# Eighteen input tiles of the even layer as split products, their low weights and the convolutions redistributed over four engines

## The chip, the cores and the metric

The kernel runs on one core of one Trainium2 chip. It is written for the engines directly: five instruction queues (TensorE, VectorE, ScalarE, GpSimd and SyncE) run in their own order and meet only at semaphores. The metric is the device time of one execution in microseconds. The kernel before takes 1738.14 us, the median of 3 runs (1737.71 to 1739.41).

## What is computed

The reference is one step of a two-layer encoder on 640 frames (a prompt of 512 frames, and 8 requests of 16 frames). The change lies in the front of the first (even) layer:

```python
proj = h @ w_in                      # h = rmsnorm(x), [640, 1024]
a_val, a_gate, z, xbc, dt_raw = split(proj)   # 512, 512, 512, 1024, 8 columns
a_glu = a_val * sigmoid(a_gate)
a_conv, new_conf_state = causal_dwconv(a_glu, conf_state, conf_w, conf_b)    # 31 taps, 512 channels
a_out = silu(layernorm(a_conv, ln_g, ln_b))
xbc_c = silu(causal_dwconv(xbc, ssd_conv_state, xbc_w, xbc_b))               # 4 taps, 1024 channels
...
y = ssd_scan(xs, dt, a, b_in, c_out, h0);  yg = y * silu(z);  b_out = rmsnorm(yg)
out = concat([a_out, b_out]) @ w_out
```

A convolution sees each request with its own carried-in frames, so the 512 prompt columns and the 8 x 16 request columns of a channel are separate pieces. The two runs over the memory tokens (keys `mk`, values `mv` of both layers) are computed between these projections.

## The kernel before

Everything lies channel-major: 128 channels on the partitions, 640 frames along them. A projection tile is 128 output channels by 640 frames, summed over 8 blocks of 128 input channels. Tiles alternate between two PSUM buffers `G[0]` and `G[1]`; `TILE` numbers them in the order of TensorE, and `begin(n)` waits until tile n-2 has been read. Weights arrive in chunks of two tiles in a ring of four slots, loaded by the SyncE queue in a fixed order.

Two kinds of product occur. `project` (called by `projections`) multiplies the f32 weights with the f32 rows `h`; each k-block takes a matmul of 512 and one of 128 columns, and the profile shows two records for each, 32 for a tile. The split product, used from `evout` tile 2 on, adds three products of rounded parts (high by high, low by high, high by low) in fp32r, 48 matmuls of 320 columns for a tile. It needs high and low parts of weights and rows: ScalarE copies to fp32r (high), and VectorE or GpSimd subtracts (low).

The order of TensorE in the stage of the change (written out by hand in `block.tensor`): the eight `glu` tiles (gate and value alternately), the narrow tile `dtp`, the four key tiles `mk1` with a statistic after each from the second on, `dt`, the two value tiles `mv1`, the eight `xbc` tiles with `conv_stat(3)` after the sixth, two `z` tiles, `conv_stat(6)`, the tile `tok`, two more `z` tiles, and the scan. All 22 tiles of glu, xbc, z and the narrow ones read `h`.

VectorE (`block.vector`) forms the four gated blocks (L2446, L2447), and in between the taps of the 31-tap convolution in `conv_taps`: for each channel block and tap one `scalar_tensor_tensor` on the 512 prompt columns and one on the 128 request columns, accumulating in `acc` in SBUF (L2434). Two instructions that follow each other never depend on each other; each waits for the one two before it. After that come `conv_sum` (L2463), the four taps of the `xbc` convolution per block (L2515, L2518) in `tmp`, again in both pieces, `subtract_mean`, and `decay_sums` (L2473 to L2496). ScalarE applies the silu of each `xbc` block (`xbc_silu`, which releases `tmp`), reads the `xbc` tiles (`xbc_rows`), the `z` tiles (`z_gate`), and works through the key statistics in `head_norms`. GpSimd scales the keys (`memory_keys`, L779 and L781) and stores the carried-out convolution states (L761).

## Time and profile before

| what | value |
|---|---|
| time, median of 3 runs | 1738.14 us (1737.71 to 1739.41) |
| span of the profiled execution | 1735.7 us |
| TensorE busy | 1702.0 us, 98% |
| VectorE busy | 1058.7 us, 61% |
| ScalarE busy | 683.9 us, 39% |
| GpSimd busy | 370.5 us, 21% |
| granted TensorE clock, mean | 1.000 |

The span runs from the first to the last instruction of one execution; 2.4 us of the median lie outside of it. Busy times are unions over the span. The length of an instruction in a row is from its start to its end, and on ScalarE and VectorE the next may start before that end, so a run of n instructions in one row gives their pitch: the row's length less the last one's, over n-1.

### The profile page before, as it was taken

How to read it: one execution, taken by the hardware profiler on the slowest of the kernel's cores; microseconds unless marked ns; L12 is line 12 of the kernel's file. 1: busy time of each engine (PE TensorE's matmuls, PEld its weight loads, DVE VectorE, ACT ScalarE, POOL GpSimd, SP SyncE). 2: the span in 40 equal slices, each digit the busy share in tenths (PEclk: the TensorE clock that was granted, in tenths of full speed). 3: DMA queues.
4: the chain of work that ended last, by engine and by line, in shares of the span. 5: the costliest groups of instructions: out<-in, count | busy, mean ns of one | idle time of the engine just before them, and what ended most of it. 6: DMA issues, size and time to landing. Idle time of an engine off the chain costs nothing.

```text
span 1735.7 us, 27688 instructions
## 1 busy us (share of the span) xinstructions
PE 1702.0 (98%) x11360; PEld 1543.0 (89%) x11360; DVE 1058.7 (61%) x1717; ACT 683.9 (39%) x1219; POOL 370.5 (21%) x289
## 2 busy tenths in 40 slices
PE   7999998999999999999999999999999999999999
PEld 6566556797999999999989899789899999999999
DVE  3699867637667647465654424744676774655574
ACT  4111243435525525253552124633543453544352
POOL 3012100211104324132213132200110241414240
PEclk9999999999999999999999999999999999999999
DMA  8222330142303131403143221603320313122212
GB/s 263 101 77 103 93 107 28 49 195 98 104 27 138 32 130 46 135 19 128 31 141 74 75 73 64 246 27 114 153 93 25 128 48 115 61 70 86 87 66 91
DMA packets 39674, 162.30 MB, mean 94 GB/s; under 512 B 9384, under 2 KB 10280, under 8 KB 25600
## 3 DMA queue, kind: packets, MB, share of 16 engines
q1 hardware_dynamic: 32240, 124.59, 21.5%
q0 software_dynamic: 7312, 35.98, 5.8%
q8 instruction: 89, 1.46, 0.4%
q14 instruction: 33, 0.27, 0.0%
HBM read 149.87 MB, written 10.42 MB: 92 GB/s over the span
## 4 chain that ended last, share of the span: by engine, by line
PE 92%; DVE 5%; ACT 2%; issue 1%; DMA 0%; POOL 0%; SPq 0%; DVEq 0%; ACTq 0%
PE G L940 68%; PE S L940 11%; PE Q L940 11%; PE Q L1635 1%; ACT work L1731 0%; DVE rstd L2344 0%; DMA ring<-in_w_mk 0%; DVE ev_low L2593 0%; ACT rstd L1731 0%; DVE stats L2623 0%; DVE resid L2875 0%; ACT h_split L1731 0%; PE Q L1347 0%; DVE stats L2992 0%; DVE work L2636 0%
## 5 line engine op out<-in xcount | busy, mean ns | idle before, releaser
L940 PE MATMUL G<-ffn_rows,w_split 128*128 128x320 f32 x2160 | 329.8, 309 | 0.0
L940 PEld LDWEIGHTS G<-ffn_rows,w_split 128*128 128x128 f32 x2160 | 320.1, 188 | 0.0
L1731 ACT ACTIVATE w_split<-ring 128x512 fp32r<-128x512 f32 (+2 forms) x224 | 159.1, 711 | 316.8 <-PE G L940 208.4
L940 PE MATMUL G<-front,ring 128*128 128x128 f32 (+2 forms) x832 | 223.3, 430 | 11.0 <-DMA ring<-in_w_mk 9.3
L940 PEld LDWEIGHTS G<-front,ring 128*128 128x128 f32 x832 | 133.0, 193 | 100.0 <-issue 95.9
L856 POOL TENSOR_TENSOR mkT<-ring 128x512 f32<-128x512 f32 x72 | 98.2, 1369 | 564.6 <-DMA ring<-in_w_up 382.2
L940 PE MATMUL G<-h_split,w_split 128*128 128x320 f32 x1344 | 200.9, 310 | 1.2 <-DVE w_split L2359 0.8
L940 PEld LDWEIGHTS G<-h_split,w_split 128*128 128x128 f32 x1344 | 197.5, 188 | 1.9 <-issue 1.3
L940 PE MATMUL G<-g_split,w_split 128*128 128x320 f32 x1056 | 163.7, 310 | 0.1
L940 PEld LDWEIGHTS G<-g_split,w_split 128*128 128x128 f32 x1056 | 156.7, 188 | 1.7 <-DVE w_split L2848 1.4
L2715 DVE TENSOR_TENSOR w_split<-ring,w_split 128x512 fp32r<-128x512 f32 (+1 forms) x124 | 105.8, 854 | 59.9 <-ACT w_split L1731 58.7
L2848 DVE TENSOR_TENSOR w_split<-ring,w_split 128x512 fp32r<-128x512 f32 (+1 forms) x80 | 66.9, 837 | 115.5 <-ACT w_split L1731 114.7
L2434 DVE SCALAR_TENSOR_TENSOR front<-front,par 128x512 f32<-128x512 f32 x240 | 113.6, 549 | 0.1
L1731 ACT ACTIVATE work<-G 128x320 f32<-128x320 f32 (+1 forms) x116 | 53.0, 457 | 141.2 <-PE G L940 138.5
L2715 DVE TENSOR_TENSOR w_split<-mv,w_split 128x512 fp32r<-128x512 f32 x72 | 50.4, 700 | 54.9 <-ACT w_split L1731 54.9
L940 PE MATMUL S<-g_split,w_split 128*128 128x320 f32 x528 | 82.1, 309 | 0.5 <-DVE w_split L2848 0.5
L940 PE MATMUL Q<-g_split,w_split 128*128 128x320 f32 x528 | 81.1, 309 | 0.1
L1731 ACT ACTIVATE front<-G 128x640 f32<-128x640 f32 (+3 forms) x44 | 24.4, 573 | 142.0 <-PE G L940 142.0
L940 PEld LDWEIGHTS S<-g_split,w_split 128*128 128x128 f32 x528 | 78.5, 188 | 0.8 <-DVE w_split L2848 0.8
L940 PEld LDWEIGHTS Q<-g_split,w_split 128*128 128x128 f32 x528 | 78.3, 188 | 0.3 <-DVE w_split L2848 0.3
L870 POOL TENSOR_TENSOR w_split<-ring,w_split 128x1024 fp32r<-128x1024 f32 x18 | 43.5, 2415 | 121.9 <-ACT w_split L1731 121.9
L940 PE MATMUL S<-ffn_rows,w_split 128*128 128x320 f32 x432 | 69.2, 309 | 0.0
(351 smaller groups left out, 2818.8 us busy)
## 6 DMA issues: line engine op xcount, KB each, us to landing
ring<-in_w_up SPq DMA_DIRECT2D x44, 1024.0 KB, 4.8
ring<-in_w_down SPq DMA_DIRECT2D x48, 256.0 KB, 2.6
ring<-in_w_down SPq DMA_DIRECT2D x32, 320.0 KB, 2.9
front<-in_mem_k POOLq DMA_DIRECT2D x8, 1024.0 KB, 6.1
front<-in_mem_v POOLq DMA_DIRECT2D x8, 1024.0 KB, 10.6
ring<-in_w_mk SPq DMA_DIRECT2D x4, 1024.0 KB, 5.9
ring<-in_w_mv SPq DMA_DIRECT2D x4, 1024.0 KB, 10.9
ring<-in_w_glu SPq DMA_DIRECT2D x4, 1024.0 KB, 8.6
```

Source lines behind the costliest of these rows:

```text
L856: nc.gpsimd.tensor_tensor(wsum[n], a, b, ALU.subtract).then_inc(sum_ready, 1)
L870: nc.gpsimd.tensor_tensor(lo, src, hi.bitcast(F32), ALU.subtract).then_inc(split, 1)
L940: return nc.tensor.matmul(out, lhsT, rhs, start=start, stop=stop, **kw)
L1635: m = nc.tensor.transpose(Q[0:z - a, e, a:a + P], fP[it % 2][:, e, a:z], ident)
L1731: return nc.scalar.activation(*a, **k)
L2434: ins = v.scalar_tensor_tensor(out=out, in0=src, scalar=tap, in1=out, op0=ALU.mult, op1=ALU.add)
L2715: v.tensor_tensor(lo, src, hi.bitcast(F32), ALU.subtract).then_inc(op_low, 1)
L2848: v.tensor_tensor(lo, src, hi.bitcast(F32), ALU.subtract).then_inc(split, 1)
```

## The change

- **Split tiles.** `FRONT` lists 18 tiles: the last six `glu` tiles, all `xbc`, all `z`, numbered q = 0 to 17. `front_product(q)` computes them as split products. The first two `glu` tiles and `dtp` stay as they were, and `dtp` moves ahead of the six. The high rows `in_hi` are a ScalarE copy of `h` into the room of the residual `x`; the low rows are `h - in_hi`, on VectorE, in place of `h`, after `dtp` has read it. `x` is fetched again from HBM by the SyncE queue after the last `z` tile (four transfers), and the residual sum of `evout` waits for it (`x_back`).
- **Weights.** For each q ScalarE copies the high weights (`front_high`, 128x1024; from q = 2 on it waits for product q-2), and VectorE subtracts the low ones in the ring (`front_low`). Both stand at fixed places of their queues, and TensorE waits for `in_low`.
- **Prompt columns.** VectorE's taps on the 512 prompt columns now accumulate in two PSUM banks (`conv_out`), even taps in one and odd taps in the other, with one more instruction for each channel block that adds the two (`PAIR_TAPS` = 32 entries a block, 128 in all). The `xbc` taps take two blocks at a time, each in its bank.
- **Request columns.** For each tap ScalarE multiplies the four channel blocks (four activations of 128 columns, with the tap as scale) into one of two buffers, and GpSimd adds the 4x128 columns into `acc` or `xbcc` (`run_sum`). Tap 0 is written by ScalarE alone. This is 31 taps for the first convolution and 2 x 4 for the second. The silu of the request columns is one ScalarE instruction for each four blocks.
- **Stores.** The `xbc` states are stored from the SyncE queue instead of GpSimd's, between the loads of `z` and `evout` weights.

The core of the diff:

```diff
+FRONT = [(name, j) for name, js in (("glu", range(2, 8)), ("xbc", range(8)), ("z", range(4))) for j in js]
+def front_tile(q):
+    name, j = FRONT[q]
+    return {"glu": glu_tile, "xbc": xbc_tile, "z": z_tile}[name](j)
+PAIR_TAPS = CW + 1
+EARLY_TAPS = (1, 1, 1, 1, 5, 4)
+STEP_TAPS = (3, 3, 3, 3, 3, 3)
...
+            def front_product(q, halfway=None):
+                n = front_tile(q)
+                begin(n)
+                out = GF[n % 2]
+                pe.wait_ge(in_low, q + 1)
+                _, w_hi, w_lo = front_piece(q)
+                steps = [(k, part) for k in range(KD) for part in (0, 1, 2)]
+                if q == 0:
+                    steps = [(k, part) for k in range(KD) for part in (0, 1)] + [(k, 2) for k in range(KD)]
+                for at, (k, part) in enumerate(steps):
+                    if q == 0 and part != 1:
+                        pe.wait_ge(in_rows_lo if part else in_rows_hi, k + 1)
+                    w, rhs = ((w_hi, in_hi), (w_lo, in_hi), (w_hi, ev_lo))[part]
+                    for f in range(2):
+                        fr = slice(f * HT, (f + 1) * HT)
+                        m = mm(out[:, fr], w[:, k, :], rhs[:, k, fr], at == 0, at == len(steps) - 1)
+                    if halfway is not None and at == len(steps) // 2 - 1:
+                        m.then_inc(halfway, 1)
+                m.then_inc(tile_done, 1)
+            s = chunk(CHUNK["glu"])
+            for n in range(2):
+                project(glu_tile(n), s, n * P, KD, rows(h), normed=None if n else APPLIED["mix0"] - KD + 1)
             narrow(TILE0["dtp"], "wdt", h)
+            for q in range(6):
+                front_product(q)
...
+            for q in range(6, 14):
+                front_product(q)
+            conv_stat(3)
+            for q in range(14, 16):
+                front_product(q)
...
+            for k in range(KD):
+                act.wait_ge(applied, APPLIED["mix0"] - KD + 1 + k)
+                A(in_hi[:, k, :], h[:, k, :], ACT.Copy).then_inc(in_rows_hi, 1)
...
+                if q >= 2:
+                    tile_wait(act, front_tile(q - 2))
+                act.wait_ge(chunk_in[c % RING], 16 * (c // RING + 1))
+                src, hi, _ = front_piece(q)
+                A(hi, src, ACT.Copy).then_inc(in_high, 1)
...
+            def run_product(out, src, scale):
+                for i in range(4):
+                    m = A(runs(out[:, i]), src(i), ACT.Copy, scale=scale(i))
+                m.then_inc(run_tap, 1)
+            def buffer_free():
+                e = products[0] = products[0] + 1
+                if e > 2:
+                    act.wait_ge(run_add, e - 2)
+                return prod[:, e % 2]
+            def conv_products(first, count):
+                for w in range(first, first + count):
+                    src = lambda j: padded(aglu, j, 0, CPROMPT, CREQ, w)[1]
+                    if w == 0:
+                        act.wait_ge(pads_in, 16 * 12)
+                        read_wait(act, glu_tile(7))
+                        for j in range(4):
+                            A(runs(acc[:, j, SEQ:T]), src(j), ACT.Identity, scale=pr("cw", j * CW), bias=pr("cb", j))
+                    else:
+                        run_product(buffer_free(), src, lambda j: pr("cw", j * CW + w))
...
+            head_norms(lambda j: mkT[:, 1, j, :], TILE0["mk1"], 4, 1.0 / P, MT,
+                       after=lambda j: conv_products(sum(EARLY_TAPS[:j]), EARLY_TAPS[j]))
+            for q in (6, 7):
+                front_high(q)
+            for m2 in range(2):
+                conv_products(sum(EARLY_TAPS[:4 + m2]), EARLY_TAPS[4 + m2])
+                memory_values(1, m2)
...
+            def xbc_run_silu(g):
+                act.wait_ge(run_add, CW - 1 + (XW - 1) * (g + 1))
+                rows = xbcc[:, 4 * g:4 * g + 4, SEQ:T]
+                A(rows, rows, ACT.Silu).then_inc(run_silu, 1)
...
+            taps = sum(EARLY_TAPS)
+            for j, count in enumerate(STEP_TAPS):
                 xbc_rows(j)
-            for j in range(2):
+                front_high(8 + j)
+                count = min(count, CW - taps)
+                conv_products(taps, count)
+                taps += count
+                if j >= 4:
+                    for i in range(2 * j - 8, 2 * j - 6):
+                        xbc_silu(i)
+            xbc_products(0)
+            xbc_rows(6)
+            front_high(14)
+            xbc_rows(7)
+            front_high(15)
+            xbc_products(1)
+            for j in range(4, 6):
                 xbc_silu(j)
+            xbc_run_silu(0)
...
+            def run_sum(out):
+                e = added_taps[0] = added_taps[0] + 1
+                pool.wait_ge(run_tap, e)
+                if e > 1:
+                    pool.wait_ge(run_add, e - 1)
+                nc.gpsimd.tensor_tensor(out, out, prod[:, e % 2], ALU.add).then_inc(run_add, 1)
...
+            for i in range(MH):
+                memory_keys(1, i, i + 1)
+                conv_sums(EARLY_TAPS[i] - (i == 0))
+            conv_sums(sum(EARLY_TAPS[4:]))
+            for j, count in enumerate(STEP_TAPS):
+                conv_sums(count if j < len(STEP_TAPS) - 1 else CW - 1 - added_taps[0])
+            xbc_sums(0)
+            pool.wait_ge(early_outs, 16 * EARLY_OUTS)
+            pool.wait_ge(xbc0_out, 16 * 2)
+            pool.wait_ge(conv, 4 * PAIR_TAPS)
+            pool.wait_ge(xbc_done, 1)
+            pool.dma_start(h0T, dram["ssd_state"]).then_inc(state_in, 16)
+            xbc_sums(1)
...
+                    j, w = at // PAIR_TAPS, at % PAIR_TAPS
+                    if w == CW:
+                        dve.wait_ge(conv, at)
+                        v.tensor_tensor(acc[:, j, 0:SEQ], acc[:, j, 0:SEQ], conv_out[1], ALU.add).then_inc(conv, 1)
+                        continue
+                    if at >= 2:
+                        dve.wait_ge(conv, at - 1)
+                    src, tap, out = aglu[:, j, w:w + SEQ], pr("cw", j * CW + w), conv_out[w % 2]
                     if w == 0:
                         ins = v.tensor_scalar(out, src, tap, pr("cb", j), ALU.mult, ALU.add)
+                    elif w == 1:
+                        ins = v.tensor_scalar(out, src, tap, None, ALU.mult)
                     else:
-                        dve.wait_ge(conv, at - 1)
-                        ins = v.scalar_tensor_tensor(out=out, in0=src, scalar=tap, in1=out,
-                                                     op0=ALU.mult, op1=ALU.add)
+                        ins = v.scalar_tensor_tensor(out=acc[:, j, 0:SEQ] if w == CW - 1 else out, in0=src, scalar=tap,
+                                                     in1=out, op0=ALU.mult, op1=ALU.add)
...
+            def front_low(q):
+                dve.wait_ge(in_high, q + 1)
+                src, hi, lo = front_piece(q)
+                v.tensor_tensor(lo, src, hi.bitcast(F32), ALU.subtract).then_inc(in_low, 1)
             dve.wait_ge(pads_in, 16 * 12)
             dve.wait_ge(small_ready, 3)
+            for q in range(2):
+                front_low(q)
             for j in range(4):
-                n = TILE0["glu"] + 2 * j
+                n, value = glu_tile(2 * j), glu_tile(2 * j + 1)
                 read_wait(dve, n)
-                tile_wait(dve, n + 1)
+                tile_wait(dve, value)
                 a, b = padded(aglu, j, CW - 1, CPROMPT, CREQ, CW - 1)
-                v.tensor_tensor(a, tmp[:, j % 2, 0:SEQ], G[(n + 1) % 2][:, 0:SEQ], ALU.mult)
-                v.tensor_tensor(b, runs(tmp[:, j % 2, SEQ:T]), runs(G[(n + 1) % 2][:, SEQ:T]), ALU.mult)\
-                    .then_inc(read[(n + 1) % 2], 1)
-                read_wait(dve, n + 1)
-                conv_taps(32 if j < 3 else 44)
+                src = (GF if j else G)[value % 2]
+                v.tensor_tensor(a, tmp[:, j % 2, 0:SEQ], src[:, 0:SEQ], ALU.mult)
+                v.tensor_tensor(b, runs(tmp[:, j % 2, SEQ:T]), runs(src[:, SEQ:T]), ALU.mult)\
+                    .then_inc(read[value % 2], 1)
+                if j == 0:
+                    tile_wait(dve, TILE0["dtp"])
+                    for k in range(KD):
+                        dve.wait_ge(in_rows_hi, k + 1)
+                        v.tensor_tensor(ev_lo[:, k, :], h[:, k, :], in_hi[:, k, :].bitcast(F32), ALU.subtract)\
+                            .then_inc(in_rows_lo, 1)
+                read_wait(dve, value)
+                if 0 < j < 3:
+                    front_low(2 * j + 1)
+                conv_taps((7, 10, 10, 16)[j])
+                if j < 2:
+                    front_low(2 * j + 2)
+                    conv_taps((7, 8)[j])
+                elif j == 2:
+                    conv_taps(8)
+            for q in (6, 7):
+                front_low(q)
             step_sizes()
-            conv_taps(8 * CW - taps_done[0])
+            conv_taps(18)
+            front_low(8)
+            conv_taps(10)
+            front_low(9)
+            conv_taps(4 * PAIR_TAPS - taps_done[0])
...
+            for pair in range(KD // 2):
+                front_low(10 + pair)
+                if pair == 3:
+                    front_low(14)
+                    conv_sum(0, conv_done, lambda k: acc[:, k, :])
                     decay_sums()
-                    conv_sum(3, lambda k: dve.wait_ge(sq_ready, 24 + k + 1), lambda k: sq[:, k % 2, :])
-                read_wait(dve, xbc_tile(j))
-                if j >= 2:
-                    dve.wait_ge(xbc_done, j - 1)
-                out = (tmp[:, j % 2, 0:SEQ], runs(tmp[:, j % 2, SEQ:T]))
+                    front_low(15)
                 for w in range(XW):
                     for i in range(2):
-                        src = padded(xbcp, j, 0, XPROMPT, XREQ, w)[i]
+                        j, out = 2 * pair + i, conv_out[i]
+                        src = xbcp[:, j, w:w + SEQ]
                         if w == 0:
-                            ins = v.tensor_scalar(out[i], src, pr("xw", j * XW), pr("xb", j), ALU.mult, ALU.add)
+                            read_wait(dve, xbc_tile(j))
+                            if pair:
+                                dve.wait_ge(xbc_done, j - 1)
+                            else:
+                                dve.wait_ge(conv, 4 * PAIR_TAPS)
+                            ins = v.tensor_scalar(out, src, pr("xw", j * XW), pr("xb", j), ALU.mult, ALU.add)
                         else:
                             dve.wait_ge(xconv, done - 1)
-                            ins = v.scalar_tensor_tensor(out=out[i], in0=src, scalar=pr("xw", j * XW + w),
-                                                         in1=out[i], op0=ALU.mult, op1=ALU.add)
+                            ins = v.scalar_tensor_tensor(out=out, in0=src, scalar=pr("xw", j * XW + w), in1=out,
...
+            subtract_mean()
+            front_low(16)
+            conv_sum(3, lambda k: dve.wait_ge(sq_ready, 24 + k + 1), lambda k: sq[:, k % 2, :])
+            front_low(17)
...
+                if c == CHUNK["evout"] + 3:
+                    tile_wait(sp, z_tile(3))
+                    for k in range(0, KD, 2):
+                        sp.dma_start(x[:, k:k + 2, :], dram["x"][:, k:k + 2, :]).then_inc(x_back, 16)
```

## Rows read from the trace of the kernel before

**Rows 1.** The page, part 1: busy us (share of the span) xinstructions

```profile
PE 1702.0 (98%) x11360; PEld 1543.0 (89%) x11360; DVE 1058.7 (61%) x1717; ACT 683.9 (39%) x1219; POOL 370.5 (21%) x289
```

**Rows 2.** TensorE's timeline: start us, us, line op names, xcount [idle before]

```profile
47.69 69.46 PE L940 MATMUL G<-front,ring 128*128 128x512 f32 x256
...
135.63 0.70 PE L940 MATMUL Q<-work,const 128*128 128x256 f32 x2 [0.85 <-ACT rstd L1731]
...
259.71 0.63 PE L1152 MATMUL G<-const,front 128*128 128x128 f32 x4 [0.99 <-ACT front L1731]
```

**Rows 3.** Chain of waits: start us, us, what (plain tiles, split tile)

```profile
204.52 34.61 PE G L940 x128
...
467.47 7.04 PE S L940 x48
```

**Rows 4.** VectorE's timeline: taps, first and last of decay_sums, a low weight

```profile
67.00 13.96 DVE L2434 SCALAR_TENSOR_TENSOR front<-front,par 128x512 f32<-128x512 f32 x30
...
130.87 0.34 DVE L2434 SCALAR_TENSOR_TENSOR front<-front,par 128x128 f32<-128x128 f32 x1
...
216.32 0.16 DVE L2473 CAST hot<-const 128x8 fp32r<-128x8 f32 x1
...
223.31 0.87 DVE L2496 TENSOR_TENSOR front<-front,csend 8x512 f32<-8x512 f32 x2
...
362.40 1.22 DVE L2359 TENSOR_TENSOR front_r<-ring,front_r 128x1024 fp32r<-128x1024 f32 x1
```

**Rows 5.** Timelines of VectorE (DVE) and GpSimd (POOL), alone and together

```profile
68.85 0.75 DVE L2434 SCALAR_TENSOR_TENSOR front<-front,par 128x512 f32<-128x512 f32 x1
...
132.42 1.25 DVE L2434 SCALAR_TENSOR_TENSOR front<-front,par 128x512 f32<-128x512 f32 x1
...
311.27 6.62 DVE L2593 TENSOR_TENSOR ev_low<-front,ev_high 128x640 fp32r<-128x640 f32 x3
...
318.55 0.81 DVE L2323 TENSOR_TENSOR resid<-resid,G 128x640 f32<-128x640 f32 x1
319.29 2.28 DVE L2593 TENSOR_TENSOR ev_low<-front,ev_high 128x640 fp32r<-128x640 f32 x3
...
310.67 5.81 POOL L815 TENSOR_TENSOR ring_split<-ring,ev_weights 128x1024 fp32r<-128x1024 f32 x2 [14.38 <-ACT ev_weights L1731]
```

**Rows 6.** ScalarE's timeline: tile read, table load, scaled and plain copies

```profile
160.26 0.77 ACT L1731 ACTIVATE front<-G 128x512 f32<-128x512 f32 x2 [6.54 <-PE G L940]
...
204.26 1.28 ACT L1731 ACT_TABLE_LOAD   x1
...
290.57 0.85 ACT L1731 ACTIVATE front<-G,const 128x256 f32<-128x256 f32 x2
...
309.54 1.99 ACT L1731 ACTIVATE ev_weights<-ring 128x1024 fp32r<-128x1024 f32 x2
311.44 2.60 ACT L1731 ACTIVATE ev_high<-front 128x640 fp32r<-128x640 f32 x4
...
319.39 0.83 ACT L1731 ACTIVATE front_r<-resid,par 128x640 fp32r<-128x640 f32 x1 [5.36 <-DVE resid L2323]
320.13 0.73 ACT L1731 ACTIVATE work<-resid 128x640 f32<-128x640 f32 x1
```

**Rows 7.** GpSimd: a key scaled (timeline), 512-column subtractions (groups of instructions)

```profile
31.88 0.72 POOL L779 TENSOR_TENSOR mkT<-mkT,rstd 128x256 f32<-128x256 f32 x1 [0.49 <-ACT rstd L1731]
32.70 0.48 POOL L781 TENSOR_SCALAR mkT<-mkT,par 128x256 f32<-128x256 f32 x1
...
L856 POOL TENSOR_TENSOR mkT<-ring 128x512 f32<-128x512 f32 x72 | 98.2, 1369 | 564.6 <-DMA ring<-in_w_up 382.2 <-DVE w_split L2715 182.3
```

**Rows 8.** TensorE (timeline), and a stretch: busy us by engine, PEclk, DMA, GB/s

```profile
9.27 9.89 PE L940 MATMUL G<-front,ring 128*128 128x256 f32 x32 [9.27 <-DMA ring<-in_w_mk]
...
33.70 7.07 PE L940 MATMUL G<-ring,front 128*128 128x256 f32 x32
...
9.00:14.00 5.00, 4.74 (x11) 3.87 (x12) 2.48 (x7) 2.39 (x6) 0.00 (x0) 1.00 1.02 420
```

More of the change, by code:

```diff
@@ L80 @@
 TILE = {}
-for _n, _c in (("mk0", 4), ("mv0", 2), ("glu", 8), ("dtp", 1), ("mk1", 4), ("dt", 1), ("mv1", 2), ("xbc", 8),
+for _n, _c in (("mk0", 4), ("mv0", 2), ("glua", 2), ("dtp", 1), ("glub", 6), ("mk1", 4), ("dt", 1), ("mv1", 2), ("xbc", 8),
                ("za", 2), ("tok", 1), ("zb", 2), ("evout", 8),
@@ L1120, in _ @@
             memory_values(1)
-            projections("xbc", 8, KD, rows(h), after=lambda n: n == 5 and conv_stat(3))
-            s = chunk(CHUNK["z"])
-            for n in range(2):
-                project(z_tile(n), s, n % 2 * P, KD, rows(h))
-            nready[0] += 4
-            conv_stat(6)
+            for q in range(6, 14):
[3 more added lines that the diff above has]
+                front_product(q)
             n = TILE0["tok"]
@@ L1138, in _ @@
                 .then_inc(tile_done, 1)
-            s = chunk(CHUNK["z"] + 1)
-            for n in range(2, 4):
-                project(z_tile(n), s, n % 2 * P, KD, rows(h), halfway=h_free if n == 3 else None)
+            front_product(16)
+            nready[0] += 4
+            conv_stat(6)
+            front_product(17, halfway=h_free)
             RUN, CSK = NCH - 1, 64 + NH
@@ L1932, in _ @@
             nc.scalar.preload_act_table_set("silu_and_others")
+            for j in range(6, KD):
+                xbc_silu(j)
+            xbc_run_silu(1)
+            act.wait_ge(applied, APPLIED["mean"])
+            for k in range(4):
+                square(acc[:, k, :])
             z_gate(1)
-            xbc_silu(5)
+            front_high(17)
             log_exp_table()
-            inv_std(1, 1.0 / CONF, eps=1)
             n = TILE0["tok"]
```

137 lines of the change are left out of this document (83 added, 54 removed).

## The prediction

> **What bounds the kernel now.** I read the shares on the page first: TensorE is busy 98% of the span [rows 1], so only what shortens TensorE's work, or leaves it waiting, moves the time. VectorE's 61% there is an average; in its own timeline of the front stage tap follows tap [rows 4]. TensorE's timeline shows the front stage as one block: it starts at 47.69, its one wait worth a name up to the last z tile is 0.85 us for the last key statistic at 135.63, and the scan starts at 259.71 [rows 2]. Everything the change does lies between those ends; the scan and all behind it keep their instructions. So I forecast the new start of the scan.
>
> **What it removes from TensorE.** In the chain of waits four plain tiles take 34.61 us, 8.65 each; a split tile takes 7.04 [rows 3]. 18 tiles x 1.61 = **29.0 us less**, all on the path. If nothing else waits, the scan starts at 230.7.
>
> **What VectorE then has to do.** 15 pairs of taps take 13.96 us, 0.93 a pair; the instruction on 128 columns takes 0.27 of it (start 130.87, next start 131.14), so one on 512 columns takes 0.66 [rows 4]. The change drops the 0.27 from each pair. It adds 18 low weights: one of this shape and kind is 1.22 long, its pitch at best 1.15 (the next starts about 0.07 before an end) [rows 4]. The 8 low rows take 0.735 each ((2.28 - 0.81) / 2: the row at 319.29 prints a run of three 128x640 subtractions, and one is 0.81 long) [rows 5].
>
> Two prices are not in the trace. *First, a tap that accumulates in PSUM.* No row has VectorE writing PSUM. The nearest are the same instruction in SBUF, 0.66, and from below a subtraction or addition of 512 columns, whose share is 0.60 (0.735 less 128 columns at 1.04 ns each, which is the difference of the two tap lengths, 0.66 - 0.27, over 384) [rows 4, 5]. I take 0.66 for taps 0 and 1 too, and 0.60 to 0.73 as bounds, the upper as far above as the lower is below. *Second, the low weights beside GpSimd's new sums.* Where a GpSimd subtraction ran, VectorE's subtractions with both inputs in SBUF took 3.0 us each (the run of three is 6.62 long with the third free), against 0.81 alone, and a tap 1.25 against 0.75 [rows 5]. Sums are in flight for about half of the time; I take 1.3 for a low weight, bounds 1.15 and 2.0.
>
> The rows say only that two SBUF inputs collide. The Trainium skill (SBUF, State Buffer; section "Who interferes with whom") says that a VectorE instruction with at most one SBUF tensor input doesn't contend with GpSimd, and one with two does; by that rule the taps, now with one input in PSUM, are free of the 36 sums, and the low weights are not. The same skill (VectorE: DVE Perf Modes, section on the TRN2 errata) charges a PSUM source 120 cycles where SBUF pays 58; by that the 44 taps below would cost 2.8 us more. The trace speaks against it: the residual sum from `G` at 318.55 is 0.81 long and the next starts 0.74 later, as among the SBUF subtractions beside it [rows 5].
>
> **ScalarE and GpSimd.** Two activations of 256 columns with a scale from a tensor take 0.85, pitch 0.36 [rows 6]; less 128 columns at 0.83 ns (1024 against 640 columns, pitch 0.95 against 0.64) that is 0.25 out of PSUM. One of 640 columns from SBUF with such a scale has pitch 0.74 (319.39 to 320.13), which gives 0.31 for 128. I take 0.31, so a tap's four products take 1.24 (1.0 to 1.5). 39 taps make 48 us, and with 18 high weights at 0.95 and 8 high rows at 0.64, 22 us, there is room on the engine, but each stands in front of something. A GpSimd sum of 512 columns is 1.37 on the mean [rows 7], 36 of them 49 us over some 100: not a bound, but the second product after it waits for it.
>
> **Where the new waits fall.** Five places, each from its queue order:
>
> 1. *Last key statistic.* Let T be the end of the fourth mk1 tile. From the end of the third, T - 3.9, ScalarE does an evacuation 0.4, a product 1.2, a square 0.4 and the inverse of the second statistic 0.9: T - 1.0. GpSimd scales that key, 0.72 + 0.48 [rows 7], and only then adds tap 1: T + 1.7. Product 3 uses that buffer: T + 3.0; square, logarithm: T + 3.9. TensorE wants it at T + 0.4. Wait 3.5, against 0.85 before [rows 2]: **+2.6**.
> 2. *Second mk1 tile* needs the fourth gated block read. VectorE from the end of `dtp` (47.69 + 2 x 8.65 + 2.4 = 67.4): low rows 5.9, four low weights 5.2, 50 entries of the taps 33.0, two gated products 1.7 (0.60 and 0.27 by the shares above), the fourth itself 0.9: 114.1. TensorE (67.4 + 6 x 7.04 + 3.5 for a key tile, which is half of the row at 33.70) is there at 113.1 [rows 8]: **+1.0**.
> 3. *Product 10, the big one.* After product 6 ends, ScalarE reads that tile (0.75), copies high weights 8 (0.95) [rows 6]; VectorE has been idle for them. Then come low 8, 10 taps, low 9, the 34 entries that are left (128 - 66 - 18 - 10), and only then low 10: 1.8 + 3 x 1.3 + 44 x 0.66 = 34.7. TensorE has three tiles to do in that time, 21.1. **+13.6.** That the engine has enough time on the mean doesn't help: low 10 is queued behind 44 entries, and it idled before them, some 7 us for high 6 behind the key norms and 6 for high 8.
> 4. *Product 12.* From the end of product 10: read 0.75, high 12 0.95, three products 3.7, table load 1.28, silu 0.6, which frees the bank; then 8 xbc taps 5.3 and low 12 1.3: 13.9, less product 11, 7.04: **+6.9**. VectorE sits idle for 8 us of it.
> 5. *Product 16.* From the end of product 12: read and high 14 1.7, low 14 1.3, the three sums 2.3, `decay_sums` 7.9 (216.32 to 224.18), low 15 1.3, 8 taps 5.3, four subtractions 3.0, low 16 1.3, a sum 0.75, two squares and the gate of z tile 1, whose buffer product 16 needs, 1.9: 26.7. TensorE: three tiles, a statistic, `tok`: 23.4. **+3.3.**
>
> Sum 27.4: nearly all of the 29.0 is handed back. Two edits I cost at nothing: the second load of `x` (2.6 MB after about 255, wanted for the sum at 318.55 before [rows 5]; if that cover were gone, it would be its own 10 us or so) and the states stored by SyncE, each issued after its chunk's slot is free, with the weights behind them not wanted for tens of us. Request columns end long before the scan.
>
> **What a long wait costs beyond itself.** TensorE's first 32 matmuls, after 9.27 us of nothing, took 9.89 us; 32 of the same shape later took 7.07 [rows 8]. The granted clock reads 1.00 in that first stretch, so that view doesn't tell; the number of matmuls done does (11 in its first 5 us, where 32 take 7.07 later). So a restart from idle costs 2.8, and I charge it for the waits of 13.6 and 6.9 and not for those under 5: **+5.6**. The Trainium skill (TensorE: Matmul & The Clock Gate, Part 1) states that the array idles at 1.2 GHz and is released to 2.4 GHz by activity; by it both waits restart at the lower level, and without it the sum is 5.6 less.
>
> Sum: -29.0 + 27.4 + 5.6 = **+4.0**. Against the profiled execution 1735.7 + 4.0 = 1739.7, and 2.4 us outside the span: **1742.1 us**.
>
> **The rivals.**
>
> *A. Restarts are free, terms as above.* -1.6 us: 1736.5. For it: the granted clock never falls below 1.00 [rows 8]. Against it: the first matmuls. With low weights at 1.6 it is about 1739. Chance 0.28.
>
> *B. Faster: VectorE is quicker than its rows.* Taps at 0.60, low weights at 1.15, products at 1.0, restarts free: term 2 goes (1.0), 3 becomes 10.5 (44 x 0.06 and 3 x 0.15 less), 1, 4 and 5 lose 2.7 together: -8, 1730 us. It decides from about 0.61 a tap on, if restarts are free. Against it: no row has this instruction below 0.66. That VectorE never makes TensorE wait, 1709 us, would take taps of 0.36; excluded. Chance 0.20.
>
> *C. Much slower: the sums hold VectorE.* If PSUM doesn't free the taps of the collision, each sum in flight lengthens a tap by 0.5 (1.25 against 0.75) [rows 5]; about 15 sums lie in the stretches of terms 2 to 4, and the low weights go to 2.0 (six of them on the path, +4): +8 to +12 on the forecast, 1751 to 1755. It decides from the first sum, and GpSimd's own rows would be longer than 1.4 too. Chance 0.10.
>
> *D. Forecast:* 0.42, its own range 1739 to 1748.
>
> **How the numbers follow.** A difference of 0.2%, 3.5 us, is about what can be told from none: below 1734.7 is faster, above 1741.6 slower. B lies below; A within; C above; of the forecast four fifths lie above (0.34) and the rest within (0.08). Some 0.02 of A falls below. Faster 0.22, same 0.34, slower 0.44. The range 1731 to 1753 leaves out the far half of B and of C, and the bounds of the tap (0.60 and 0.73 move the sum by -5 and +7) lie in it.
>
> **What would show each step.** After: split tiles in the front of 7.04; taps of 512 columns at a pitch of 0.66 with no 128-column partner; TensorE idle behind `DVE ring_split` (the low weights) for some 13 us around 172 to 186, and for 7 us around 200 to 207; matmuls of the split tiles longer than 310 ns right behind these waits; a wait of 3.5 at the last key statistic; the scan's first transposes at about 264 instead of 259.71; from there to the end nothing changed. Wrong would be: a tap pitch under 0.62, no wait at product 10, or a longer stretch behind the scan's start (a wait for `x`).

## The result: 1746.5 us, 0.5% slower, and the profile after

The changed kernel takes 1746.47 us (median of 4 runs, 1745.01 to 1747.38), the kernel before 1738.33 (4 runs beside it); the ratio is 1.0047, with a 95% interval of 1.0033 to 1.0060. Forecast were 1742.1 and a range of 1731 to 1753. The profiled execution has a span of 1745.2 us against 1735.7.

The page, part 1 (busy us, share of the span, instructions) and the line of the granted clock in part 2; it answers to [rows 1]:

```profile
PE 1681.2 (96%) x11648; PEld 1588.6 (91%) x11648; DVE 1047.9 (60%) x1591; ACT 757.0 (43%) x1405; POOL 407.5 (23%) x309
...
PEclk9999699999999999999999999999999999999999
```

TensorE is busy 20.8 us less than in [rows 1], and the span is 9.5 us longer. One digit of the clock line is a 6: the fifth slice, 175 to 218 us. TensorE's timeline, whose last bracket is the idle time before a row and what ended it, shows the waits; it answers to [rows 2]:

```profile
113.85 0.92 PE L1008 MATMUL G<-front,ring 128*128 128x256 f32 x3 [0.78 <-DVE front L2640]
...
128.83 1.22 PE L1008 MATMUL Q<-work,const 128*128 128x256 f32 x2 [3.05 <-ACT rstd L1825]
...
145.85 0.64 PE L1008 MATMUL G<-resid_high,in_weights 128*128 128x320 f32 x2
...
187.82 0.87 PE L1008 MATMUL G<-resid_high,in_weights 128*128 128x320 f32 x2 [13.67 <-DVE ring_split L2627]
...
212.38 0.87 PE L1008 MATMUL G<-resid_high,in_weights 128*128 128x320 f32 x2 [7.81 <-DVE ring_split L2627]
...
250.09 0.90 PE L1008 MATMUL G<-resid_high,in_weights 128*128 128x320 f32 x2 [4.29 <-ACT front L1825]
...
268.64 0.63 PE L1245 MATMUL G<-const,front 128*128 128x128 f32 x4 [1.06 <-ACT front L1825]
```

The five rows with a wait ahead of the last one are the five places of the prediction, in order of time: second mk1 tile, last key statistic, products 10, 12 and 16. The row at 145.85 is the start of product 6. One small wait was not forecast: 0.66 us for low 15, ahead of product 15 at 237.57. The scan starts at 268.64 instead of 259.71 [rows 2], 8.93 us later. Behind it the idle times of TensorE are those of before, and the rest of the span is 0.6 us longer. So the whole question lies between 47 and 269 us.

What VectorE does ahead of product 10 (its timeline; L2627 is the low weight, L2618 the tap):

```profile
131.99 2.75 DVE L2627 TENSOR_TENSOR ring_split<-ring,in_weights 128x1024 fp32r<-128x1024 f32 x2 [7.40 <-ACT in_weights L1825]
...
136.84 11.93 DVE L2618 SCALAR_TENSOR_TENSOR S<-front,par,S 128x512 f32<-128x512 f32 x18
155.03 1.23 DVE L2627 TENSOR_TENSOR ring_split<-ring,in_weights 128x1024 fp32r<-128x1024 f32 x1 [6.26 <-ACT in_weights L1825]
156.17 6.68 DVE L2618 SCALAR_TENSOR_TENSOR S<-front,par,S 128x512 f32<-128x512 f32 x10
162.76 1.22 DVE L2627 TENSOR_TENSOR ring_split<-ring,in_weights 128x1024 fp32r<-128x1024 f32 x1
...
166.64 18.52 DVE L2618 SCALAR_TENSOR_TENSOR S<-front,par,S 128x512 f32<-128x512 f32 x28
...
186.45 1.22 DVE L2627 TENSOR_TENSOR ring_split<-ring,in_weights 128x1024 fp32r<-128x1024 f32 x1
```

This is step 3 of the prediction, row by row: low 6 and 7 after 7.40 us of idleness, low 8 after 6.26, ten taps, low 9, 34 entries, low 10. 28 taps in 18.52 us are a pitch of (18.52 - 0.75) / 27 = 0.658.

```profile
128.00:134.00 6.00, 5.17 (x15) 0.72 0.25 107
134.00:140.00 6.00, 6.00 (x30) 1.00 0.00 0
...
187.00:190.00 3.00, 2.18 (x8) 0.50 0.00 0
190.00:193.00 3.00, 3.00 (x13) 0.50 0.00 0
193.00:196.00 3.00, 3.00 (x21) 0.93 0.00 0
...
212.00:216.00 4.00, 3.62 (x14) 0.50 0.03 4
...
250.00:252.00 2.00, 1.91 (x7) 0.50 0.00 0
```

Behind four waits the clock is at its lower level: that of 13.67 us, of 7.81, of 4.29, and, seen in 0.72 between 128 and 134 us, the one of 3.05 as well.

### The profile page after: what moved, and what is told of

The parts are those of the page before. It is cut to its first block, busy times and chain, and to the rows that moved or that the text cites. A ratio compares the mean times of both kernels' runs of the same rounds, so it can differ in the third digit from the quotient of the medians.

```text
span 1745.2 us, 28430 instructions
## 1 busy us (share of the span) xinstructions
PE 1681.2 (96%) x11648; PEld 1588.6 (91%) x11648; DVE 1047.9 (60%) x1591; ACT 757.0 (43%) x1405; POOL 407.5 (23%) x309
## 4 chain that ended last, share of the span: by engine, by line
PE 85%; DVE 9%; ACT 4%; issue 1%; DMA 0%; POOL 0%; SPq 0%; DVEq 0%; ACTq 0%
PE G L1008 62%; PE S L1008 11%; PE Q L1008 11%; DVE S L2618 3%; ACT front L1825 1%; ACT work L1825 1%; PE Q L1729 1%; ACT rstd L1825 1%; DVE ring_split L2627 0%; DVE rstd L2523 0%; DMA ring<-in_w_mk 0%; DVE ev_low L2815 0%; DVE stats L2845 0%; DVE resid L3097 0%; ACT h_split L1825 0%
## 5 line engine op out<-in xcount | busy, mean ns | idle before, releaser
L1008 PE MATMUL G<-ffn_rows,w_split 128*128 128x320 f32 x2160 | 329.8, 309 | 0.0
L1008 PEld LDWEIGHTS G<-ffn_rows,w_split 128*128 128x128 f32 x2160 | 320.1, 188 | 0.0
L1008 PE MATMUL G<-h_split,w_split 128*128 128x320 f32 x1344 | 200.9, 310 | 1.2 <-DVE w_split L2538 0.8
L1008 PEld LDWEIGHTS G<-h_split,w_split 128*128 128x128 f32 x1344 | 197.5, 188 | 1.9 <-issue 1.3
L1008 PE MATMUL G<-g_split,w_split 128*128 128x320 f32 x1056 | 163.7, 310 | 0.1
L1008 PEld LDWEIGHTS G<-g_split,w_split 128*128 128x128 f32 x1056 | 156.7, 188 | 1.6 <-DVE w_split L3070 1.4
L1008 PE MATMUL G<-resid_high,in_weights 128*128 128x320 f32 x288 | 69.5, 324 | 26.4 <-DVE ring_split L2627 22.1
L1008 PE MATMUL S<-g_split,w_split 128*128 128x320 f32 x528 | 82.1, 309 | 0.5 <-DVE w_split L3070 0.5
L1008 PE MATMUL Q<-g_split,w_split 128*128 128x320 f32 x528 | 81.1, 309 | 0.1
L1008 PEld LDWEIGHTS S<-g_split,w_split 128*128 128x128 f32 x528 | 78.5, 188 | 0.8 <-DVE w_split L3070 0.8
L1008 PEld LDWEIGHTS Q<-g_split,w_split 128*128 128x128 f32 x528 | 78.3, 188 | 0.3 <-DVE w_split L3070 0.3
L1008 PE MATMUL G<-front,ring 128*128 128x256 f32 (+2 forms) x256 | 65.9, 415 | 11.8 <-DMA ring<-in_w_mk 9.3
L1008 PEld LDWEIGHTS G<-resid_high,in_weights 128*128 128x128 f32 x288 | 50.5, 198 | 27.5 <-issue 23.0
L2618 DVE SCALAR_TENSOR_TENSOR S<-front,par,S 128x512 f32<-128x512 f32 x112 | 74.5, 748 | 0.0
L1008 PEld LDWEIGHTS G<-front,ring 128*128 128x128 f32 x256 | 44.9, 195 | 31.7 <-issue 26.9
```

The source lines that it names most:

```text
L1008: return nc.tensor.matmul(out, lhsT, rhs, start=start, stop=stop, **kw)
L2618: ins = v.scalar_tensor_tensor(out=acc[:, j, 0:SEQ] if w == CW - 1 else out, in0=src, scalar=tap, in1=out, op0=ALU.mult, op1=ALU.add)
```

## The experiments

Each run is the changed kernel with the edit shown, or, where it says so, an earlier experiment with one more edit. The kernel before took 1737.8 to 1738.1 us beside them. Line numbers shift by the edit.

### 1. TensorE kept busy in the waits

```diff
+            def keep_busy(count):
+                pe.wait_ge(stat_read, nstat[0])
+                for _ in range(count):
+                    mm(QF[:, 0:HT], in_hi[:, 0, 0:P], in_hi[:, 0, 0:HT], True, True)
...
             for q in range(6, 14):
+                keep_busy({10: 84, 12: 44}.get(q, 0))
                 front_product(q)
...
+            keep_busy(20)
             front_product(16)
```

> The changed kernel, with matmuls that nobody reads put in front of products 10, 12 and 16 (84, 44 and 20 of 320 columns, 12.3, 6.5 and 2.9 us at 0.147 each, a little less than the waits of 13.67, 7.81 and 4.29 us). The waits stay; only TensorE is busy in them. Theory (a wait of over 4 us is followed by matmuls at half the pitch, at a granted clock of 0.50): product 10 takes 7.04 instead of 9.79, products 12 and 13 14.1 instead of 16.46, product 16 7.04 instead of 9.43, the scan starts 7.5 us earlier (261.1) and the time is about 1739. Rival (the slow tiles come from something else that happens behind these waits, weights or VectorE's and ScalarE's traffic): no change, 1746.5.

Measured: 1740.52 us (ratio to before 1.0014, interval 1.0004 to 1.0024), scan start 263.10. The timeline ahead of product 10, and the stretch behind it:

```profile
175.28 12.48 PE L1008 MATMUL Q<-resid_high 128*128 128x320 f32 x84
189.12 0.39 PE L1008 MATMUL G<-resid_high,in_weights 128*128 128x320 f32 x1 [1.35 <-DVE ring_split L2635]
...
188.00:191.00 3.00, 1.88 (x13) 1.00 0.03 5
```

The work is the same and comes no earlier, only TensorE was busy until 1.35 us before it, and the clock stays at 1.00. Products 10 and 12 then take 7.06 us from start to start, against 9.61 and 9.31 without the filling; product 16 with the statistic behind it takes 8.09 against 10.26. So these waits cost 2.5, 2.2 and 2.2 us beyond their length, and the cause is TensorE's idleness. The time fell by 5.9 instead of 7.5 because these three give 7.0 and the restart behind the last key statistic, which this edit doesn't touch, happened to be 1.5 longer here: 18.5 us from the start of that statistic to product 6, against 17.0 (128.83 to 145.85 in the changed kernel). The Trainium skill (TensorE: Matmul & The Clock Gate, Part 1) says that the array idles at 1.2 GHz and activity releases it; the trace agrees, with 0.50 behind the wait of 13.67 us and 1.00 with filler in it.

### 2. The columns moved, the tiles not split

```diff
 def front_product(q): ...
-                for at, (k, part) in enumerate(steps): ...
+                for k in range(KD):
+                    for f in range(2):
+                        m = mm(out[:, fr], src[:, k, :], h[:, k, fr], k == 0, k == KD - 1)
 front_high, front_low, in_hi, low rows:
-                ...
```

> The changed kernel with its 18 tiles computed as before, from the unsplit rows and weights (8 x 2 matmuls of 320 columns each); high and low rows and weights aren't made at all. What is left of the change is the taps on 512 columns, the request columns on ScalarE and GpSimd, and the moved stores. Theory (the split saves 29.0 us of TensorE, and all long waits are waits for low weights): no wait at products 10, 12 and 16, only the one at the last key statistic (3 us instead of 0.85), scan start at about 262, time 1740 to 1742. Rival (moving the request columns itself holds TensorE back, by late states or late gates): waits of several us stay before the z tiles or the scan, 1746 or more.

Measured: 1742.87 us (ratio 1.0031, 1.0019 to 1.0042). The long waits are gone; TensorE's timeline has left

```profile
137.40 1.22 PE L1008 MATMUL Q<-work,const 128*128 128x256 f32 x2 [3.05 <-ACT rstd L1820]
154.64 69.07 PE L1008 MATMUL G<-front,ring 128*128 128x320 f32 x256
244.69 8.88 PE L1008 MATMUL G<-front,ring 128*128 128x320 f32 x32 [1.66 <-ACT front L1820]
264.25 0.63 PE L1240 MATMUL G<-const,front 128*128 128x128 f32 x4 [0.99 <-ACT front L1820]
```

Moving the request columns off VectorE is no gain by itself. 4.5 us are lost up to the scan: 2.2 at the last key statistic, 1.5 for its restart and 1.66 for a late z gate, less some 0.7, since a plain tile takes 8.61 us here in matmuls of 320 columns (the eight `xbc` tiles start at 154.64, the statistic behind them at 223.55) and 8.65 before in matmuls of 512 and 128. And the run measures the split: it starts the scan 4.39 us before the changed kernel, which has 27.2 us of waits (13.67, 7.81, 4.29, 0.78, 0.66) and 7.0 of restarts more and 1.66 less. 27.2 + 7.0 - 1.66 - 4.39 = 28.15; with 18 x 0.04 = 0.7 for the shorter plain tiles it is 28.9. The 29.0 us that the split saves TensorE are real, and all of them are spent on waiting.

### 3. Half of the taps back in SBUF

```diff
-                    src, tap, out = aglu[:, j, w:w + SEQ], pr("cw", j * CW + w), conv_out[w % 2]
+                    src, tap = aglu[:, j, w:w + SEQ], pr("cw", j * CW + w)
+                    out = conv_out[1] if w % 2 else acc[:, j, 0:SEQ]
```

> The changed kernel, with the even taps of the first convolution accumulated in SBUF (in acc) and the odd ones in PSUM as before: half of VectorE's taps have two SBUF inputs again, beside the same GpSimd sums. Theory (two SBUF inputs collide with GpSimd, one doesn't): even taps that run beside a sum are 1.25 long, alone 0.75, odd ones 0.75 throughout; of the 44 entries of the taps before product 10 some ten get 0.5 longer, the wait there grows from 13.7 to about 18, time 1750 to 1754. Rival (where the tap accumulates doesn't matter at these rates): every tap at a pitch of 0.66, 1746.5.

Measured: 1751.27 us (ratio 1.0075, 1.0059 to 1.0092); the wait at product 10 is 19.39. GpSimd's row and four taps of VectorE's beside and behind it (`front` is SBUF, `S` PSUM):

```profile
156.08 5.21 POOL L841 TENSOR_TENSOR front<-front 128x512 f32<-128x512 f32 x3 [4.19 <-ACT front L1825]
...
157.30 1.13 DVE L2619 SCALAR_TENSOR_TENSOR front<-front,par 128x512 f32<-128x512 f32 x1
158.35 0.74 DVE L2619 SCALAR_TENSOR_TENSOR S<-front,par,S 128x512 f32<-128x512 f32 x1
...
162.42 0.74 DVE L2619 SCALAR_TENSOR_TENSOR front<-front,par 128x512 f32<-128x512 f32 x1
163.08 0.74 DVE L2619 SCALAR_TENSOR_TENSOR S<-front,par,S 128x512 f32<-128x512 f32 x1
```

A tap that accumulates in SBUF takes 1.13 in these rows beside a sum (the lengthened ones up to product 10 are 1.09 to 1.78) and 0.74 alone; its neighbour in PSUM takes 0.74 in both cases. GpSimd's three sums take 5.21 here and 4.17 in the changed kernel. The rule of the Trainium skill that the prediction weighed (SBUF, State Buffer; "Who interferes with whom") is borne out, and with it rival C falls: the two PSUM banks do protect the taps.

### 4. The same instructions in another order

`conv_taps`, `front_low`, `front_high` and the rest are issued from two lists, one token a step, in place of the fixed places:

```diff
+SCALAR_ORDER = """
+tap*2 high*2 tap*2 value tap*8 value tap*2 row tap high tap*2 high row tap*5 row high*2 tap*2 row tap
+high dt silu*2 row tap row high silu*2 tap*2 state*2 high silu state silu state row*2 high mean state*2
+run_silu state*2 high gate decay silu*2 run_silu gate high squares tok gate var gate mix"""
+VECTOR_ORDER = """
+tap*10 step_sizes tap*6 low tap*6 low tap*17 low tap*5 low tap*12 low tap*3 low tap*3 state*8 low state*9
+low state*7 total low decay_sums low state*8 low subtract squares low scale"""
-EARLY_TAPS = (1, 1, 1, 1, 5, 4)
+EARLY_TAPS = (1, 1, 1, 0, 5, 4)
```

> The changed kernel with the same instructions in another order on VectorE and ScalarE (GpSimd's sums follow): low weights 8, 9, 10, 11 placed among the taps, each at the place that VectorE reaches as its high weight is there, the states' taps of the second convolution between the lows 11 to 16, high weights 6 and 7 after two taps' products, no product before the last key statistic. Theory (VectorE has time enough on the whole; the waits come from what each low weight is queued behind): all waits over 1.5 us in front of the scan go, and with them the three restarts: 28.6 - 2 + 7.5 us less, scan start at about 234, time 1712 (1709 to 1718). Rival (VectorE is short of time in this stage, so another order only moves the waits, to the z tiles or to the last states): 1730 or more.

Measured: **1721.52 us**, ratio 0.9905 (0.9889 to 0.9922): 25 us below the changed kernel and 16 below the one before, though 3.5 above the end of the range expected. Scan start 239.56 instead of 234. The waits for products 10, 12 and 16 are gone. One came in their place, and one in the scan. TensorE, then the VectorE rows ahead of the first, then the ScalarE rows ahead of the second:

```profile
212.35 0.60 PE L1023 MATMUL G<-resid_high,in_weights 128*128 128x320 f32 x1 [4.73 <-DVE ring_split L2646]
245.28 0.33 PE L1260 MATMUL G<-const,front 128*128 128x128 f32 x1 [3.11 <-ACT front L1840]
...
197.95 2.29 DVE L2646 TENSOR_TENSOR ring_split<-ring,in_weights 128x1024 fp32r<-128x1024 f32 x1
206.35 1.47 DVE L2708 CAST cs_parts<-front 8x640 bf16<-8x640 f32 x1
...
239.20 3.35 ACT L1840 ACTIVATE front<-front,par 128x640 f32<-128x640 f32 x4
242.57 1.28 ACT L1876 ACT_TABLE_LOAD   x1
```

Low weights and parts of `decay_sums` run beside GpSimd's sums here and are longer: a low weight 2.29 instead of 1.22, `decay_sums` 11 us instead of 7.9 (product 15 waits behind it). And the four silus `mix` stand behind the last z gate, with the scan's first copies behind them.

### 5. One low weight moved

```diff
             front_low(9)
+            conv_taps(14)
+            front_low(10)
             conv_taps(4 * PAIR_TAPS - taps_done[0])
...
-                front_low(10 + pair)
+                if pair:
+                    front_low(10 + pair)
```

> The changed kernel with one low weight moved: low 10 comes 14 entries of the taps after low 9 instead of 34, low 11 stays behind the taps and the states' first 8 taps. Theory (a low weight is late by what it is queued behind, and the next one takes the wait over): no wait at product 10; low 11 is ready when it was, so product 11 waits some 12 to 13 us and the time stays within 2 us of 1746.5. Rival (what counts is that low 10 is late behind 44 entries, and product 11 and later ones have slack): the wait of 13.7 goes with its restart, about 1730.

Measured: 1744.67 us (ratio 1.0044, 1.0027 to 1.0060). TensorE's rows for products 10, 11 and 13:

```profile
175.50 0.39 PE L1008 MATMUL G<-resid_high,in_weights 128*128 128x320 f32 x1 [1.42 <-DVE ring_split L2627]
195.44 0.61 PE L1008 MATMUL G<-resid_high,in_weights 128*128 128x320 f32 x1 [12.72 <-DVE ring_split L2627]
218.33 0.61 PE L1008 MATMUL G<-resid_high,in_weights 128*128 128x320 f32 x1 [6.28 <-DVE ring_split L2627]
```

The wait goes where the next low weight stands behind the taps: low 11 behind the rest of the taps and the states' first eight. The wait of 7.81 went the same way, from product 12 to product 13, whose low weight stands behind taps that VectorE idles 9.45 us for.

### 6. Two low weights moved

As in 5, with low 10 and low 11 each behind ten more entries.

> The changed kernel with low 10 and low 11 moved among the taps (10 entries after low 9 and 10 after low 10). Theory: both products find their low weights; product 12 still waits for low 12, since that follows the states' first taps and these the first silus on ScalarE, 7 to 8 us, product 16 4 to 5 us. The 13.7 us and their restart of 2.75 go, less some 2 us: scan start at 254 to 256, time 1731 to 1734, below the kernel before. Rival (VectorE is short of time, so the wait moves to product 12 or 13 in full): 1744 or more.

Measured: 1737.22 us (ratio 0.9995, 0.9985 to 1.0004), the time of before; the expectation was 3 to 6 us too low. Product 12 waits twice what I had expected. Its row, and the chain of waits ahead of it:

```profile
203.35 0.61 PE L1008 MATMUL G<-resid_high,in_weights 128*128 128x320 f32 x1 [14.87 <-DVE ring_split L2627]
...
181.11 7.91 DVE S L2618 x12
...
192.03 3.95 DVE S L2740 x6
...
197.58 3.95 DVE S L2740 x6
201.53 1.68 DVE ring_split L2627
```

I had followed ScalarE's silus only. Low 12 stands behind 14 entries of the taps and 16 taps of the states, 20 us with no wait over 0.7, and each low weight of this stretch takes 1.76 to 1.97 beside the sums. So part of the rival was right: with two low weights moved, VectorE's work itself holds the third.

### 7. The silus ahead of the last gate

On top of 4:

```diff
-run_silu state*2 high gate decay silu*2 run_silu gate high squares tok gate var gate mix"""
+run_silu state*2 high gate decay silu*2 run_silu gate high squares tok gate var mix gate"""
```

> The run with the new order on both engines (1721.5), with one swap on ScalarE: the four silus of the first convolution (mix) ahead of the last z gate, as in the changed kernel, not behind it. In that run they and a table load stood between the last z tile and the first copies of the scan, whose second chunk of transposes waited 3.11 us instead of 0.74. Theory: this wait goes back to 0.74 and its restart too, time 1718 (1717.5 to 1719.5). Rival (that wait has another cause): 1721.5.

Measured: 1717.74 us (ratio 0.9886, 0.9869 to 0.9902), as the theory had it; the wait in the scan is 0.74.

### 8. `decay_sums` in two parts

A further order on both engines, with low 15 between the two parts and `mix` ahead of the gate (the last low weights of `VECTOR_ORDER`: `state*7 total decay_sums low state decay_parts low state*8 low subtract low squares scale`).

> A further order of the same instructions on VectorE and ScalarE: decay_sums in two parts with low 15 handled between them, mix ahead of the last gate. In the run with the new order product 14 or 15 waited 4.73 us for a low weight behind decay_sums, which took 11 us beside GpSimd's last sums instead of 8. Theory: no wait over 1.5 us and no restart in front of the scan, scan start at 232 to 236, time 1709 to 1714. Rival (VectorE's operations with two SBUF inputs beside the sums take so much longer that another product waits): 1716 or more.

Measured: **1717.11 us** (ratio 0.9883, 0.9866 to 0.9899), no better than 7 and above the 1709 to 1714 expected. Scan start 238.93. The longest wait up to there, and the stretch from 67 to 200 us (busy us of TensorE, weight load, VectorE, ScalarE, GpSimd; clock):

```profile
206.78 0.39 PE L1023 MATMUL G<-resid_high,in_weights 128*128 128x320 f32 x1 [2.88 <-DVE ring_split L2646]
...
207.21 0.47 DVE L2709 CAST cs_parts<-front 8x640 bf16<-8x640 f32 x1
...
67.00:200.00 133.00, 127.78 (x806) 121.34 (x799) 131.66 (x182) 76.64 (x198) 54.71 (x48) 1.00 0.31 91
```

VectorE is busy 131.66 of 133 us, and TensorE waits 0.9 to 2.9 us in five places (1.6 of it at the scan's start, for ScalarE), with no restart (clock 1.00). I read this as a stage bound by VectorE, but no run shows that, and three numbers speak against it. The busy time isn't fixed: the low weights here are 1.6 to 2.2 long where a sum runs and 1.21 where none does. Behind 200 us, where the longest wait lies, VectorE is busy only 28.31 of the 39 us to 239. And run 4, with VectorE busy 130.71 of the same 133 us, has product 14 running at 200.39, 6.4 us earlier than here (206.78). Run 4's order up to there with run 8's behind it was not tried.

### 9. The product behind the fourth key tile

```diff
-EARLY_TAPS = (1, 1, 1, 1, 5, 4)
+EARLY_TAPS = (1, 1, 1, 0, 6, 4)
```

> The changed kernel with one product moved: no tap's product on ScalarE behind the fourth mk1 tile, one more at the first mv1 tile. Theory (the wait of 3.05 us for the last key statistic comes from that product, which waits for a GpSimd sum; and this wait too is followed by TensorE below its full clock, 0.72 between 128 and 134 us, which costs 1.2 to 2.5 us more): the wait falls to 0.85, the span from the last key statistic to product 6 from 16.4 to 15.2 us, later waits for low weights give part back: time 1742.5 to 1745. Rival (products 10 and 12 are paced by VectorE's queue, which doesn't start earlier by this): VectorE's low 10 comes as late as before, 1745.5 to 1747.

Measured: 1742.66 us (ratio 1.0026, 1.0016 to 1.0037), 3.8 less than the changed kernel. The wait is 0.85, the clock between 128 and 134 us is 1.00, and from the last key statistic to product 6 it is 15.5 us instead of 17.0. Product 10 waits 13.67 us as before, to the hundredth, and starts 3.8 us earlier: its queue hangs on the end of product 6, not on an absolute time. That the times differ by the same 3.8 is partly chance: the profiled execution takes 1741.33 against 1747.01 and starts the scan 5.7 us earlier (262.98), since its restarts are cheaper too. Product 10 behind the same wait, in the chain of waits, against `187.82 9.79 PE G L1008 x48` in the changed kernel:

```profile
184.05 8.75 PE G L1008 x48
```

### 10. A third order

The orders worked out again with 1.8 us for low weights beside sums; `decay_sums` came behind five taps of the states that follow low 14, its second part behind three more.

> One more order of the same instructions, worked out with low weights beside GpSimd's sums at 1.8 us (measured 1.5 to 2.2) instead of 1.2. Theory (this stage is now bound by VectorE, whose sum of work leaves no idle time between 67 us and the last z tiles): 1714 to 1718, no better than the two orders at 1717. Rival (the order is what still holds it back): below 1713.

Measured: 1721.90 us (ratio 0.9905, 0.9890 to 0.9920), outside of the expectation: the tile `tok`, which needs the decays, waits 6.38 us and restarts TensorE. It doesn't tell theory from rival, and no other run does.

## Why the prediction was right, and where not

The side, the mechanism and the five places were right, and in four of them the chain that makes the wait; the middle was 4.4 us too low (4.9 against the profiled execution, 1747.01). By its own terms:

| term | forecast | trace of after |
|---|---|---|
| 18 tiles split | -29.0 | -28.9 (run 2) |
| last key statistic | +2.6 | +2.2 |
| second mk1 tile | +1.0 | +0.8 |
| product 10 | +13.6 | +13.7 |
| product 12 | +6.9 | +7.8 |
| product 16 | +3.3 | +4.3 |
| smaller waits (product 15) | 0 | +0.7 |
| restarts (key statistic, products 10, 12, 16) | +5.6 | +8.4 (1.5, 2.5, 2.2, 2.2) |
| scan start | +4.0 | +8.9 |

The right column adds up to 9.0; the 0.1 between that and 8.9 is rounding.

*The prices.* A tap in PSUM: 0.66 forecast, 0.658 measured. A low weight: 1.3 forecast; 1.14 from start to start where no sum runs (186.45 to 187.59), and beside sums 1.59 long in the changed kernel (low 12), 1.97 in run 6 and 2.29 in run 4. So single ones lie outside of the given range (1.15 to 2.0). In the changed kernel low 10 runs alone: GpSimd has no sum between 181.2 and 200.6. A tap's four products: 1.24 forecast, 1.2 to 1.3 measured. The 2.8 us for PSUM sources, which the Trainium skill's page (VectorE: DVE Perf Modes; section on the TRN2 errata) would have added, don't appear: a tap is 0.74 long in PSUM and in SBUF alike (run 3).

*The waits.* Those at products 12 and 16 were forecast 0.9 and 1.0 too short. The chain of waits of after, first ahead of product 12 and then ahead of product 16 (start, us, what):

```profile
203.26 1.28 ACT L1825
...
210.73 1.51 DVE ring_split L2627
212.38 16.46 PE G L1008 x96
...
240.83 1.28 ACT L1861
242.12 0.74 ACT front L1825
242.88 1.28 ACT L2104
...
249.45 0.60 ACT front L1825
```

For product 12 it is the chain of the forecast, 14.8 us from the end of product 10 instead of 13.9: tenths at every step, the most (0.2 each) at low 12, which runs beside a sum, and at the three products, 3.9 instead of 3.7. For product 16 it is another chain. I had gone over VectorE, from low 14 by `decay_sums` to low 16. In the trace the last to come is mostly ScalarE, from the end of product 13 on, with one GpSimd sum (1.74) and one VectorE addition (0.84) between its pieces: high 15, the products of the states, two table loads of 1.28 around the exponential of the decays, silus, squares, and the gate of z tile 1, which frees the buffer. The table loads were not in my sum.

*The step that failed* is the size of the restarts. The 2.8 us for one was near (2.5 and 2.2 measured behind the two waits that it was charged for). "I charge it for the waits of 13.6 and 6.9 and not for those under 5" was a choice, and no row supported it: [rows 2] has a wait of 0.85 and [rows 8] one of 9.27, and nothing between. The waits of 4.29 and 3.05 were followed by a restart too: +2.2 and +1.5. With these two (3.7) and the 1.9 us of products 12 and 16 the forecast would have been 1747.7. The sentence of the prediction that the granted clock "doesn't tell" was right for the first stretch; here it does tell, with 0.50. Three slips of working changed nothing: 0.66 - 0.27 over 384 columns is 1.02 ns and not 1.04; the row read and the high copy of term 3 are 1.7 and not 1.8; and rival C's +8 to +12 is 1750 to 1754, not 1751 to 1755.

*The rivals.* A (restarts free) is refuted by run 1. B (VectorE faster) by the pitch. C (sums hold the taps) by the pitch of 0.658 too, and run 3 shows that PSUM is the reason; but for the low weights its mechanism is there, and it helps to keep the new orders at 1717 instead of the 1709 to 1714 expected. "That VectorE never makes TensorE wait, 1709 us, would take taps of 0.36" was wrong in its reason: the taps needn't be faster, the low weights need another place. The prediction treated the order as given, rightly for its question, and so it read 13.6 us of order as a price of the split.

*Cover.* The second load of `x` and the stores on SyncE cost nothing that shows: behind the scan's start the waits are the same.

## What to carry to other kernels

When work for TensorE is prepared on an engine with other long work, ask for each piece not whether the engine has time, but how many instructions stand ahead of it at the moment its input is ready; moving one piece handed the wait to the next (run 5, 1.8 us gained), moving two gained 9 (run 6), and placing all of them 25 (run 4). Count a restart for every wait of some us: here waits of 3.05 to 5.08 us cost 1.5 to 3.0 beyond their length, and keeping TensorE busy with work that nobody reads got 2.2 to 2.5 us back for each. Accumulating in PSUM kept the taps clear of GpSimd's sums here (0.74 long beside them and alone, run 3); an operation that needs two SBUF inputs is better placed where GpSimd is quiet.

## What the runs showed of the hardware that was not expected

- *Not every wait is followed by the lower clock, and the price of a restart varies.* Behind waits of 0.90 to 2.88 us (runs 1 and 8) a split tile took 7.05 to 7.07 us from start to start; behind waits of 4.29 to 19.39 us it took 8.4 to 9.9, with no relation to the length: 8.82 behind 19.39, 9.87 behind 4.73. (One of 2.22 us in run 10, shortly after one of 6.38, was followed by 9.3.) Even the same wait has no fixed price: product 10 took 9.61 behind 13.67 us in the changed kernel and 8.57 in run 9, and the 3.05 us before the value tiles cost 1.5 us in one execution, 1.6 in others, and 3.0 in run 1, where that stretch would take 15.5 undisturbed (run 9). Whether it was the length or the work ahead of it that made 2.88 us harmless in run 8 and 3.05 not is open, and so is what sets the price.
- *A cast of one SBUF input is held up too, in the one place where it ran beside the sums.* The cast of 8x640 in `decay_sums` takes 0.47 us alone (run 8) and 1.47 beside GpSimd's sums (run 4), where a tap with one SBUF input isn't held up at all. The Trainium skill (SBUF, State Buffer; "Who interferes with whom") names copies and casts among the operations that can take both port pairs; the trace agrees, 0.47 against 1.47.
